# Local key projection issued ahead of the new latent key blocks, with its weight unit ahead of the pooling units

## The reference

```python
h = rmsnorm(x, norm_mix); proj = h @ w_in
u_pool, q_b, k_b, v_b, q_lat, kv_lat, kr_raw, gates = split(proj)
y_pool = pool_mixer(u_pool, ...)            # windowed means, then a 4 x (128x128) product
qs, ks = rmsnorm(q_b), rmsnorm(k_b)         # local ("swa") queries and keys, 8 and 2 heads
y_swa  = local_attention(qs, ks, v_b, ...)
cq = rmsnorm(q_lat); qm = rope(cq @ w_qup)  # latent attention: queries
c_kv = rmsnorm(kv_lat); k_rope = rope(kr_raw)
km, vm = expand(c_kv, k_rope)               # c_kv @ w_kvup, new and cached keys
y_mla  = latent_attention(rmsnorm(qm), rmsnorm(km), vm)
x = x + (sum_i sigmoid(gate_i) * (y_i @ w_branch_i)) @ w_out
x = x + swiglu(rmsnorm(x)) @ w_down
```

## Time and profile before

| | us |
|---|---|
| median of 3 runs (1047.9 to 1048.27) | 1048.13 |
| the profiled execution | 1049.03 |
| its span, first to last instruction | 1047.1 |
| PE busy in it | 1040.9 (99%) |
| DVE, ACT, POOL busy | 635.0, 505.7, 316.7 |

### The profile page before, as it was taken

How to read it: one execution, slowest core, us unless ns; L and a number is a source line. 1 busy time by engine, 2 the same in 40 slices (tenths; PEclk the granted TensorE clock), 3 DMA queues, 4 the chain that set the end, 5 groups by cost and what they waited for, 6 DMA issues and landing times.

```text
span 1047.1 us, 20063 instructions
## 1 busy us (share of the span) xinstructions
PE 1040.9 (99%) x7594; PEld 1007.5 (96%) x7594; DVE 635.0 (61%) x1073; ACT 505.7 (48%) x926; POOL 316.7 (30%) x277
## 2 busy tenths in 40 slices
PE   9999999999999999999999999999999999999998
PEld 6899999999999999999998999999999999999998
DVE  6768764445766666543567786554557566565443
ACT  6557655444554444434354485554445444433341
POOL 3365666541121111100133745556312211111000
PEclk9999999999999999999999999999999999999999
DMA  7454534244535544454514544333355454454441
GB/s 243 120 150 126 184 103 123 84 139 141 160 118 166 160 142 158 141 179 149 176 44 137 149 145 130 100 120 121 114 152 158 122 173 146 150 150 145 156 144 69
DMA packets 48708, 146.29 MB, mean 140 GB/s; under 512 B 8801, under 2 KB 14401, under 8 KB 48641
## 3 DMA queue, kind: packets, MB, share of 16 engines
q1 hardware_dynamic: 42416, 143.05, 44.8%
q10 hardware_dynamic: 6224, 2.30, 0.9%
HBM read 142.11 MB, written 3.22 MB: 139 GB/s over the span
## 4 chain that ended last, share of the span: by engine, by line
PE 97%; DVE 1%; DMA 0%; ACT 0%; issue 0%; SPq 0%; ACTq 0%
PE psum L558 29%; PE psum L559 28%; PE psum L560 28%; PE psum L718 1%; PE psum L757 1%; PE psum L678 1%; PE psum L679 1%; PE psum L740 1%; PE psum L683 1%; PE psum L700 1%; PE psum L705 1%; PE psum L701 1%; PE psum L748 1%; PE psum L790 1%; PE psum L972 0%; PE psum L845 0%
## 5 line engine op out<-in xcount | busy, mean ns | idle before, releaser
L558 PE MATMUL psum<-AH,WH 128*128 128x320 f32 x1328 | 414.2, 312 | 0.2
L560 PE MATMUL psum<-AH,WL 128*128 128x320 f32 x1328 | 410.3, 309 | 0.0
L559 PE MATMUL psum<-AL,WH 128*128 128x320 f32 x1328 | 410.2, 309 | 0.0
L558 PEld LDWEIGHTS psum<-AH,WH 128*128 128x128 f32 x1328 | 249.3, 188 | 7.3 <-issue 5.5
L559 PEld LDWEIGHTS psum<-AL,WH 128*128 128x128 f32 x1328 | 249.4, 188 | 0.2
L560 PEld LDWEIGHTS psum<-AH,WL 128*128 128x128 f32 x1328 | 249.3, 188 | 0.0
L1055 ACT CAST WH<-raw 128x1024 fp32r<-128x1024 f32 x166 | 172.9, 1046 | 127.3 <-PE psum L560 126.0
L1483 DVE TENSOR_TENSOR WL<-raw,WH 128x1024 fp32r<-128x1024 f32 x103 | 127.6, 1240 | 114.6 <-ACT WH L1055 114.3
L1933 POOL TENSOR_TENSOR WL<-raw,WH 128x1024 fp32r<-128x1024 f32 x60 | 147.6, 2477 | 116.8 <-ACT WH L1055 98.1
L1668 DVE TENSOR_TENSOR WL<-raw,WH 128x1024 fp32r<-128x1024 f32 x88 | 107.6, 1223 | 49.6 <-ACT WH L1219 48.3
L1938 POOL TENSOR_TENSOR fab<-fa,fb 128x320 f32<-128x320 f32 x44 | 38.7, 880 | 264.7 <-DVE fb L1673 264.7
(11 more groups left out here) (268 smaller groups left out, 1578.5 us busy)
## 6 DMA issues: line engine op xcount, KB each, us to landing
raw<-w_all SPq DMA_DIRECT2D x264, 512.0 KB, 3.5
y_out<-X SPq DMA_DIRECT2D x8, 160.0 KB, 2.9
X<-x_in SPq DMA_DIRECT2D x2, 320.0 KB, 5.7
X<-x_in SPq DMA_DIRECT2D x1, 640.0 KB, 7.4
lat_out<-ckv ACTq DMA_DIRECT2D x2, 320.0 KB, 3.4
scratch<-brel SPq DMA_DIRECT2D x8, 63.8 KB, 4.3
ckv<-lat_in SPq DMA_DIRECT2D x1, 384.0 KB, 5.4
bias<-scratch SPq DMA_DIRECT2D x8, 48.0 KB, 4.5
```

The costliest lines, as they stand in the source:

```text
L558: mm(out, WH[:, slot, c0:c0 + cols], high, start=first, stop=False)
L559: mm(out, WH[:, slot, c0:c0 + cols], low, start=False, stop=False)
L560: return mm(out, WL[:, slot, c0:c0 + cols], high, start=False, stop=last)
```

## The change

It moves the local key projection SK, unit and tile, from behind the four pooling tiles to directly behind the third query-latent tile, ahead of key blocks 4 to 6. The unit numbers change with it: SK becomes 8 and the pooling units 9 to 12 (before: pooling 8 to 11, SK 12). In layer 0 the latent's square sum moves from the middle of the second query-latent tile to behind it. The loop has nine steps instead of ten. The numbers of the units that the engines split at step q stay the same (at step q, ACT and DVE take unit q + 12), while step q now belongs to the pooling tile q, SV (q = 4) or a local query (q = 5 to 8).

```diff
-U_KVK, U_KVV, U_KV, U_KR, U_QL, U_POOL, U_SK, U_SV, ... = (0, 1, 2, 4, 5, 8, 12, 13, ...)
+U_KVK, U_KVV, U_KV, U_KR, U_QL, U_SK, U_POOL, U_SV, ... = (0, 1, 2, 4, 5, 8, 9, 13, ...)
...
@@ PE, open_tile
             elif T_POOL <= t < T_POOL + 4:
-                pe.wait_ge(s.v_ready if t % 2 else s.kn_ready, l * KB + KB - (1 if t < T_POOL + 2 else 0))
+                pe.wait_ge(s.v_ready if t % 2 else s.kn_ready, l * KB + KB - (1 if t in (T_POOL, T_POOL + 3) else 0))
@@ PE, key_rows
-            elif kb != CACHED + 1:
+            elif kb == CACHED + 1:
+                pe.wait_ge(s.tile_free, l * NT + T_SK + 1)
+            else:
                 pe.wait_ge(s.kn_ready, l * KB + kb - 1)
@@ PE, main order
-            dense(l, U_QL + 1, T_QL + 1, between=(lambda: latent_sum(l)) if l == 0 else None)
+            dense(l, U_QL + 1, T_QL + 1)
+            if l == 0:
+                latent_sum(l)
             turn_rope(l, 1)
             dense(l, U_QL + 2, T_QL + 2)
+            dense(l, U_SK, T_SK)
...
-            for q in range(10):
+            for q in range(9):
                 dense(l, U_POOL + q, T_POOL + q)
-                if q == 7:
+                if q == 6:
@@ ACT
             high(l, U_QL + 2)
+            high(l, U_SK)
...
             A(SQ[:, 0:2, :], kvr[:], ACT.Square).then_inc(s.sq_kv, 1)
             root(l, N_KV, 128, T, 256)
-            high(l, U_POOL)
...
-            for q in range(10):
-                if q == 9:
+            for q in range(9):
+                if q == 8:
                     window_query(l, 3)
-                if q < 9:
-                    high(l, U_POOL + q + 1 + LEAD)
+                high(l, U_POOL + q + LEAD)
-                if q == 7:
+                if q == 6:
                     root(l, N_SWK, 128, T, 64)
-                if 6 <= q < 9:
-                    window_query(l, q - 6)
+                if 5 <= q < 8:
+                    window_query(l, q - 5)
@@ DVE
             TT(krT[64:96, 0:T], krt[64:96, 1, :], krt[64:96, 2, :], ALU.add).then_inc(s.kr_ready, 1)
+            low(l, U_SK)
             r = recip(l, N_KV, 128, T)
...
             scaled(l, T_QL + 1, qlr[:, 1, :])
-            low(l, U_POOL)
             scaled(l, T_QL + 2, qlr[:, 2, :])
+            p = full_tile(l, T_SK)
+            TT(kT[:, 0:SEQ], p[:, 0:SEQ], rstd[:, 0:SEQ], ALU.mult)
+            TT(kT[:, 384:448], p[:, SEQ:T], rstd[:, SEQ:T], ALU.mult).then_inc(s.tile_free, 1)
...
-                if q == 8:
+                if q == 7:
                     recip(l, N_SWK, 128, T)
@@ POOL
-            low(l, U_POOL + 1)
+            low(l, U_POOL)
...
-            low(l, U_POOL + 2)
+            low(l, U_POOL + 1)
...
-            low(l, U_POOL + LEAD)
+            low(l, U_POOL + 2)
```

More of the change, by code:

```diff
@@ L42 @@
 MSCALE = 1.0 / math.sqrt(QK)
-U_KVK, U_KVV, U_KV, U_KR, U_QL, U_POOL, U_SK, U_SV, U_SQ, U_PW, U_QUP, U_GATE, U_MERGE, U_OUT, U_FFN, U_DOWN = (
-    0, 1, 2, 4, 5, 8, 12, 13, 14, 18, 19, 22, 46, 58, 66, 110)
+U_KVK, U_KVV, U_KV, U_KR, U_QL, U_SK, U_POOL, U_SV, U_SQ, U_PW, U_QUP, U_GATE, U_MERGE, U_OUT, U_FFN, U_DOWN = (
+    0, 1, 2, 4, 5, 8, 9, 13, 14, 18, 19, 22, 46, 58, 66, 110)
 NU = 132
@@ L53 @@
 WARM = 4
-T_KV, T_KR, T_QL, T_POOL, T_SK, T_SV, T_SQ, T_TV, T_PY, T_Q, T_ATT, T_MERGE, T_FFN = (
-    0, 2, 3, 6, 10, 11, 12, 16, 18, 22, 30, 71, 87)
+T_KV, T_KR, T_QL, T_SK, T_POOL, T_SV, T_SQ, T_TV, T_PY, T_Q, T_ATT, T_MERGE, T_FFN = (
+    0, 2, 3, 6, 7, 11, 12, 16, 18, 22, 30, 71, 87)
 NT = 131
@@ L121, in stored @@
     l, r = divmod(u, NU)
-    return l * NU + (r + 6 if r < 2 else r - 2 if r < 8 else r)
+    return l * NU + (r + 6 if r < 2 else r - 2 if r < U_SK else 12 if r == U_SK else r - 1 if r < U_SV else r)
 VBLK = (0, 64, 128, 256, 320)
@@ L437, in used @@
             t = T_PY + 3
-        elif u >= U_POOL:
-            t = T_POOL + u - U_POOL
+        elif u >= U_SK:
+            t = T_SK + u - U_SK
         else:
@@ L1299, in _ @@
             act.dma_start(lay(kr_out).rearrange("a p n -> (a p) n"), krT[64:96, 0:T]).then_inc(s.out_rest, 16)
-            high(l, U_POOL + 1)
+            high(l, U_POOL)
             for kb in range(CACHED, KB):
@@ L1314, in _ @@
             key_columns(l, KB - 1)
-            high(l, U_POOL + LEAD)
-            for q in range(10):
-                if q == 9:
+            high(l, U_POOL + 2)
+            for q in range(9):
+                if q == 8:
                     window_query(l, 3)
-                if q < 9:
-                    high(l, U_POOL + q + 1 + LEAD)
-                if q == 5:
+                high(l, U_POOL + q + LEAD)
+                if q == 4:
                     act.wait_ge(s.tile_free, l * NT + T_POOL + 4)
@@ L1759, in _ @@
                         .then_inc(s.tile_free, 1)
[L1760 to L1764, removed]
+                elif q == 4:
+                    p = full_tile(l, T_SV)
+                    TT(vT[:, 0:SEQ], p[:, 0:SEQ], rstd[:, 0:SEQ], ALU.mult)
+                    TT(vT[:, 384:448], p[:, SEQ:T], rstd[:, SEQ:T], ALU.mult).then_inc(s.tile_free, 1)
                 else:
-                    scaled(l, T_POOL + q, qsr[:, q - 6, :])
+                    scaled(l, T_POOL + q, qsr[:, q - 5, :])
                 if q == 0:
@@ L1772, in _ @@
                     ins.then_inc(s.stat_applied, 1)
-                    dve.wait_ge(s.split_ready, l * NU + U_POOL + LEAD + 1)
+                    dve.wait_ge(s.split_ready, l * NU + U_POOL + LEAD)
                 if q < 8:
-                    low(l, U_POOL + q + 1 + LEAD)
+                    low(l, U_POOL + q + LEAD)
                 if 3 <= q < 7:
@@ L1797, in _ @@
                     TT(dL[:, g, :], tR[:, g % 3, :], dH[:, g, :].bitcast(F32), ALU.subtract).then_inc(s.d_low, 1)
-                if q == 8:
+                if q == 7:
                     recip(l, N_SWK, 128, T)
-                if q == 9 and l == 0:
+                if q == 8 and l == 0:
                     v.tensor_reduce(rq[:, 0:1], ident[:, 0:64], AX.X, ALU.add).then_inc(s.own_parts, 1)
@@ L2003, in _ @@
             g_.tensor_tensor(SQ[:, 0, :], SQ[:, 0, :], SQ[:, 1, :], ALU.add).then_inc(s.kv_sum, 1)
-            pool.wait_ge(s.split_ready, l * NU + U_POOL + 1)
-            low(l, U_POOL + 1)
+            pool.wait_ge(s.split_ready, l * NU + U_SK + 1)
+            low(l, U_POOL)
             for kb in range(CACHED, KB):
```

## The result

The changed kernel takes 1052.35 us (median of 6 executions, 1051.61 to 1055.13) against 1047.98 (6, 1047.88 to 1048.27): a ratio of 1.0043, with a 95% interval of 1.0034 to 1.0053. It is slower by 4.4 us where 4.0 was forecast. The profiled execution took 1053.0 us, its span is 1051.2.

What follows compares the result with a forecast made beforehand. PE was taken as the bound, ending the chain for 97% of the 1047.1 us span. Layer 0 +1.1 and layer 1 +2.9 gave +4.0 on 1048.13, a median of 1052.1 us, range 1050.2 to 1054.3.

Steps and rivals of the forecast that it cites:

- The gain of layer 0: Line 588 to the key blocks, layer 0: PE's waits at line 588 and key block 4 go, 1.30 us gained.
- the rotated key: PE's transposes of the rotated key, layer 0: krT becomes late next, 0.1 us given back, between 0 and 0.2.
- Line 588 in layer 1: Latent's square sum, layer 1: ACT's extra cast delays POOL's add, 0.60 us lost, 0.97 if the add keeps 1.26.
- Unit 10: Second pooling tile, both layers: PE waits for POOL's low part of unit 10, 0.2 us per layer, between 0 and 0.4.
- The end of the loop: End of q loop: later DVE and ACT splits make PE wait at three places, 2.1 us per layer, bounds 1.4 and 2.6.
- the ring's rival: Unit 23's transfer waits for POOL's split of unit 20, ACT stands there: 0.75 us more per layer, 1053.6; chance 0.14.
- The sum: All terms: layer 0 +1.1, layer 1 +2.9, together +4.0; span 1051.1 us, median 1052.1 us.
- all upper bounds at once: Every term of both layers at its upper bound together, put at +6.2 us in the prediction.

Runs made afterwards that it cites:

- e4: Kernel before with only layer 0's latent square sum moved behind the second query-latent tile, SK's tile left where it was: 1048.68 us, ratio 1.0005.
- e6: Changed kernel with ACT's high part of unit 8 put behind the latent's square instead of ahead of it: 1053.70 us, ratio 1.0051 to before.
- e10: As e9, but ACT casts units 9 and 10 behind the latent's root, as early as queues allow: 1050.49 us, ratio 1.0025 to before.
- e8: As e7, with layer 1's latent square sum also behind the second query-latent tile: 1047.49 us, ratio 0.9998 to before.
- e1: Kernel before with ACT's eight pieces of unit 20 moved behind SQ3's squares and copies: 1051.72 us, ratio 1.0029.
- e2: Kernel before with DVE's seven pieces of unit 19 moved one read-out later, behind SQ2's read-out: 1050.56 us, ratio 1.0021.
- e3: Kernel before with the moves of both e1 and e2, no tile of PE moved: 1054.73 us, ratio 1.0055.
- e7: Changed kernel with every split of units 10 to 20 one step earlier, unit 12's low part on POOL instead of DVE: 1047.89 us, ratio 1.0005 to before.
- e5: Changed kernel with ACT's eight pieces of unit 20 ahead of SQ3's squares and copies again: 1052.13 us, ratio 1.0038 to before.
- e9: e8 with POOL's split of unit 10 behind key block 4's rotation and layer 0's DVE 'own' columns behind the transposed values' copies: 1046.30 us, ratio 0.9986 to before.

## Why the prediction was right, point by point

**The gain of layer 0**: forecast 1.30 less 0.1 for the rotated key; measured 1.40 up to the first pooling tile. turn_rope's first step was 0.12 too long, as forecast. The term was 0.2 too small. That 0.2 stands behind line 588: before, the second product behind it came after 0.39 (42.28 to 42.67) where 0.15 is usual; now turn_rope stands right behind it, and nearly all of that extra is gone. And the term's reasoning had a flaw that the sum hid: e4 shows that the 0.40 of line 588 is no gain of its own but is borrowed from key block 4, and only SK's tile makes it one.

**Line 588 in layer 1**: 0.60 forecast, 0.57 measured, 0.54 by e6. The value hung on POOL's add taking 0.88 instead of 1.26; it took 0.86, and 1.26 in e6. By the Trainium skill ("SBUF — State Buffer", section "SBUF: two separate sides") the port pair that GpSimd and VectorE share is an exclusive lock, held for the whole instruction. The two ckv in e10 agree, and krm in e8 behaves the same way: each ended within 0.4 us of the end of a split on POOL.

**Unit 10**: 0.2 per layer forecast. In after the second pooling tile itself starts 0.07 (layer 1) and 0.15 (layer 0) late; another 0.21 and 0.12 come in small steps behind it, to the tile of SQ3. Together 0.28 and 0.26: the size was right, the place only in part.

**The end of the loop**: 2.1 per layer forecast, 2.06 measured in each. By step, layer 1: 0.71 in the small products (0.7), 0.58 at the fourth PY tile (0.55), 0.79 at the first query tile (0.85; 0.1 of it was there before). e1 and e2 show its two halves apart (1.34 and 0.67), e3 both, e7 the removal. This is the cause of the slowdown.

**What was not in the sum**: in layer 0 a step 0.28 too long at a gate tile (108.83). Timeline of ACT, after, where unit 23's cast waits:

```profile
105.06 1.06 ACT L1060 CAST WH<-raw 128x1024 fp32r<-128x1024 f32 x1 [0.81 <-DMA raw<-w_all]
```

That is the ring's rival, in kind as it was put (the transfer of unit 23 behind POOL's split of unit 20), but with 0.28 in one layer and not 0.75 in each; in layer 1 ACT waits 0.44 at the same place and PE not at all. e1 shows 0.56, with unit 20 as late and no other cause.

**The sum**: layer 0 +1.2 (forecast 1.1), layer 1 +2.9 (2.9), the span 1051.2 (1051.1). The median agrees with it partly by luck: the three executions at a clock of 1.000 took 1051.6 to 1051.7, 3.6 above before, the three others 1053.0 to 1055.1, and the median of 1052.35 lies between the two groups. What the second group pays was in no term of mine. The profiled execution belongs to it, and before's profiled one (1049.03, against a median of 1048.13) was a long one too: both begin slowly (last section), so that falls out between the two profiles, but not out of the medians. One sum of the prediction is wrong by its own terms: all upper bounds at once (0.2, 0.97, 0.4 twice, 2.6 twice, less 1.3) give +5.9 and not +6.2; nothing hangs on it.

## What to carry to other kernels

When a tile is moved ahead in a full engine's order, every queue that works a fixed number of units ahead has to be shifted with it; here the tile's move was worth about 1.4 us and the splits left one step late cost 4. Look behind the moved tile to the end of the stage for engines that run without a pause, and cost their whole chain once, not each wait. A free stretch in one engine's queue isn't free if its neighbour on the shared SBUF port is on the path.

## What the runs showed of the hardware

**Behind a wait among small products PE's clock often falls.** At line 945 PE has 40 products of two columns, and with the change a wait of 0.64 in their middle. In the five profiles with that wait (ten places) the granted clock fell to 0.50 (the 1.2 GHz level) a few us behind it at seven: in e2 in layer 0, in e3, e5 and e6 in both layers. It did not fall in e2's layer 1 nor in after's own profile, and at none of the fourteen places of the seven profiles without the wait. So the wait makes a fall likely; it isn't enough for one. Timeline of PE in e3 before and after the fall: the steps between products go from 0.15 to 0.27.

```profile
99.28 0.31 PE L560 MATMUL psum<-dH,WL 128*128 128x320 f32 x1
100.00 0.61 PE L558 MATMUL psum<-dH,WH 128*128 128x320 f32 x1 [0.41 <-issue]
100.40 0.47 PE L559 MATMUL psum<-dL,WH 128*128 128x320 f32 x1
100.67 0.47 PE L560 MATMUL psum<-dH,WL 128*128 128x320 f32 x1
```

What a fall costs depends on what is behind it. In e2 and e5 it is 1.3 to 1.4 us each, in layer 0 of e3 and e6 some 2 us. In layer 1 of e3 and e6 it is no more than 0.15: PE would have waited there for ACT and DVE anyway, and the slower products fill that time.

**The kernel's start is slow in some executions, and the recorded clock shows it only in part.** Timeline of PE, before, then e2: the steps between products of 512 columns are 0.43 in one and 0.23 in the other.

```profile
7.94 0.63 PE L678 MATMUL psum<-WKH,ckvH 128*128 128x512 f32 x1
8.37 0.63 PE L679 MATMUL psum<-WKH,ckvL 128*128 128x512 f32 x1
...
7.14 0.39 PE L679 MATMUL psum<-WKH,ckvL 128*128 128x512 f32 x1
7.37 0.40 PE L678 MATMUL psum<-WKH,ckvH 128*128 128x512 f32 x1
```

From the first such product to the first weight tile it is 16.7 to 17.0 us in the profiles of before, after, e1, e3, e5, e6 and e9, and 16.0 to 16.1 in those of e2, e4, e7, e8 and e10. Only after and e1 record a granted clock of 0.50 there (from 8 to 10 us in after); the other five record 1.00 beside the same steps. So a mean clock of 1.000 doesn't say that an execution began fast. It fits that three of e4's executions (1049.8 to 1050.1) and three of e8's (1048.3 to 1048.6) lie about 1 us above the rest at a clock of 1.000; they have no profile, so this stays open.

For the same reason a count of executions is a rough one. A mean clock below 1.000 was seen in after 3 of 6, e2 5 of 8, e3 5 of 5, e5 5 of 5, e6 4 of 5, in all 22 of 29, and before in 5 of 60, e4, e9 and e10 0 of 31, e8 2 of 11, e1 3 of 7, e7 5 of 11. But a slow start alone gives 0.998 (after's and e1's profiles). Below 0.998 were 14 of the 29 executions with the wait among the small products, and none of the 120 without it. Waits of 0.57 at line 588 and of 1.4 at key block 4 (e10) between full tiles brought no fall in any profile. What exactly the clock answers to was not tried.

**POOL and DVE**: a split on POOL (2.4 us) stretched DVE's ckv, which has two SBUF inputs, from 0.55 to 2.69, and krm, with 3 columns and a single input, from 0.17 to 1.23.
